# Layer 0's opening: key and rotary columns as one run of 288, in three chunks by contraction blocks

## The chip, the cores and the metric

The kernel runs on one core of a Trainium2 chip. The metric is the device time of one execution in microseconds (us); lower is better. Engines: PE multiplies matrices, DVE, ACT and POOL work on vectors, and SP issues most of the transfers from HBM, the chip's large memory. PEld is PE's loading of weights, which goes beside its matmuls.

## The reference

Two layers of a block with three parallel branches, over 256 latent tokens (x) and 256 context tokens (ctx), width 1024. Each layer scales and shifts its normalised input by vectors computed from a conditioning vector, then multiplies by one combined matrix `w_in` (1024 x 5024). The opening of layer 0 is this much of it:

```python
c_act = jax.nn.silu(c); cc_act = jax.nn.silu(c_ctx)
sh1, sc1, g1, sh2, sc2, g2 = jnp.split((c_act @ w_mod[l] + b_mod[l])[:, None, :], N_MOD, axis=-1)
mod_c = jnp.split(cc_act @ w_mod[l] + b_mod[l], N_MOD, axis=-1)
hc = modulate(rms_norm(xc, ln1_g[l]), mod_c[0], mod_c[1])
projc = hc @ w_in[l]
h = modulate(rms_norm(x, ln1_g[l]), sh1, sc1)
proj = h @ w_in[l]
# columns of proj: 0:384 queries, 384:640 keys and values (latent), 640:672 rotary key,
# 672:1184 the convolution's a and g, then the short convolution, then the gates
```

After it come attention with a rotary key, two convolution branches, a gated merge with an output projection, and a SwiGLU layer of width 2816, twice, and a last RMSNorm. Everything is float32.

## The kernel before

All activations are kept transposed, channels on the 128 partitions, the 2 x 256 tokens of both streams side by side (512 columns), in eight blocks of channels (`DT` = 8). To keep float32's accuracy a product is made of three: weights and activations are each split into a high part and a remainder, `Whi`, `Wlo`, `Hhi`, `Hlo`, and a tile gets `Whi`x`Hhi`, `Wlo`x`Hhi` and `Whi`x`Hlo` for each block.

Weights come in chunks. SP loads a chunk into one of four slots of `Wraw` (`load`, L450), ACT writes `Whi` (`split_hi`, L401), DVE writes `Wlo` (`split_lo`, L412), and PE takes it with `chunk()`. The kind of a chunk tells the two splits its shape: "plain" is 8 blocks x 128 columns, "rope" is 8 blocks x the 32 rotary columns; its high part and remainder lie side by side in `Whi`, 64 columns a block, so that one matmul makes both products (`rotation`, L2219 to L2222). A tile is one bank of PSUM, PE's output memory, 128 x 512; `tile_done` tells that it is complete.

The order of work is written out by hand, engine by engine; each engine runs its list in order, and semaphores tie the lists together. No planner is in it.

The opening computes the first vectors of the conditioning and the first tiles of the projection together. Shift and scale of the first norm are 2048 columns of `w_mod[0]`. They are taken in four parts; part p gives the vectors of the channel blocks 2p and 2p+1. A part is eight transfers of 256 KB, one for each block of the contraction, and PE multiplies them in four pairs (`first_pair`, L2379, 16 matmuls of 128 columns into `scores`). Then a serial chain: ACT copies the result as a row (`mod_row`, L824), PE turns it (`mod_turn`, L2422), DVE adds the bias (L1333), makes the gain (L1417) and the scaled input Z (L1431), ACT adds the shift and writes `Hhi` (L840), DVE writes `Hlo` (L1405). Only then can PE multiply by these two blocks.

In the time between, `opening` (from L2226) lets PE work on blocks that it has, for three tiles (two of the keys, the first of the convolution's g) and a fourth, rotary one. `high(j)` (L2235, L2236) multiplies block j's `Hhi` by `Whi` and `Wlo` of the tiles named, `low(j)` (L2242) its `Hlo` by `Whi`, `rotation` the rotary columns. `first_steps(p)` is the four pairs of part p one behind the other. After the opening come the other tiles of the projection, one by one (L2075 to L2077).

SP issues in this order: x, ctx, the two conditioning vectors, key tile 0, part 0, key tile 1, tile g, rotary columns, parts 1, 2 and 3, a table, and then the chunks of the other tiles, each as its slot comes free.

Of the kernel before, what the change touches and what calls it, by code (L numbers as in the profile page):

```python
# [17 lines left out]
P = 128  # L18
# [8 lines left out]
CW = P  # L27
# [36 lines left out]

HEAD_KINDS = ["keys", "fours", "values"]
# [98 lines left out]
def build(nc, x, c, ctx_in, c_ctx, w_mod, b_mod, ln1_g, w_in, q_a_norm_g, w_q_b, kv_a_norm_g,  # L166
# [6 lines left out]
    with stack:  # L173
# [165 lines left out]
        cond_tanh = sem("cond_tanh")  # L339
        cond_done = sem("cond_done")  # L340
        conv_a = sem("conv_a")
        conv_summed = sem("conv_summed")
# [14 lines left out]
        def parts(kind, slot):  # L357
# [81 lines left out]
        def _(sp):  # L439
# [335 lines left out]
        def _(act):  # L775
# [98 lines left out]
            act.activation(RSTD[:, :], PV[:, :], ACT.Copy).then_inc(x_norm, 1)  # L874
            look()
            mod_row(0)
            for l in range(DEPTH):
                TQ = NS[l] * SEQ
                nxt = ahead(projection_kinds(l), HEAD_KINDS)
                if l == 0:  # L880
                    next(nxt)
                    for part in range(PARTS):
                        normed_h(0, 0, 2, range(part * PART, (part + 1) * PART))
                        if part == 0:
                            look()
                            look()
# [14 lines left out]
                copy_out(TG[:, 0, 0:TQ], TQ, ACT.Tanh, 0.5)  # L901
                step_in()
                at.tile()
# [390 lines left out]
        def _(dve):  # L1294
# [230 lines left out]
            at.mod.n = TURN  # L1525
            look()
            dve.wait_ge(x_norm, 1)
            for l in range(DEPTH):
                TQ = NS[l] * SEQ
                nxt = ahead(projection_kinds(l), HEAD_KINDS)  # L1530
                if l == 0:
                    next(nxt)
                    for part in range(PARTS):
                        a, b = part * PART, (part + 1) * PART
                        mod_add_part(part)
                        gains(0, 0, LN1, 2, a, b)
                        normed_h(0, 0, 2, a, b)
                        if part == 0:
                            look()
                            look()  # L1540
                            look("rope")

# [3 lines left out]
                for j in range(2):  # L1546
                    if l or j:
                        step_in()
# [499 lines left out]
        def _(pe):  # L2048
# [163 lines left out]

            def rotation(slot, t, j, ready):

                both = Whi[:, slot, 0:DT * 2 * ROPE].rearrange("p (g n) -> p g n", g=DT)
                dst = banks[t.bank]
                pe.wait_ge(op_lo, ready + j + 1)
                if j == 0:
                    pe.matmul(dst[0:2 * ROPE, :], both[:, j, :], Hhi[:, j, :], start=True, stop=False)  # L2219
                last = pe.matmul(dst[0:ROPE, :], both[:, j, 0:ROPE], Hlo[:, j, :], start=False, stop=False)  # L2220
                if j:
                    last = pe.matmul(dst[0:2 * ROPE, :], both[:, j, :], Hhi[:, j, :], start=False, stop=j == DT - 1)  # L2222
                return last

            def opening(ready):

                slots = [chunk()]
                tiles = [new_tile() for _ in range(AHEAD)]

                def high(j, some=range(AHEAD)):  # L2230

                    pe.wait_ge(op_hi, ready + j + 1)
                    for q in some:
                        w, dst = slice(j * P, (j + 1) * P), banks[tiles[q].bank][:, :]
                        pe.matmul(dst, Whi[:, slots[q], w], Hhi[:, j, :], start=j == 0, stop=False)  # L2235
                        pe.matmul(dst, Wlo[:, slots[q], w], Hhi[:, j, :], start=False, stop=False)  # L2236

                def low(j, some=range(AHEAD)):

                    pe.wait_ge(op_lo, ready + j + 1)  # L2240
                    for q in some:
                        last = pe.matmul(banks[tiles[q].bank][:, :], Whi[:, slots[q], j * P:(j + 1) * P], Hlo[:, j, :],  # L2242
                                         start=False, stop=j == DT - 1)
                    return last

                high(0, [0])
                high(1, [0])
                low(0, [0])
                low(1, [0])
                first_pair(1, 0)  # L2250
                slots.append(chunk())
                high(0, [1])
                first_pair(1, 1)
                high(1, [1])
                first_pair(1, 2)
                slots.append(chunk())
                high(0, [2])
                first_pair(1, 3)
                low(0, [1, 2])
                mod_turn(1)  # L2260
                high(1, [2])
                low(1, [1, 2])
                slot, t = chunk(), new_tile()
                rotation(slot, t, 0, ready)
                rotation(slot, t, 1, ready)
                high(2)
# [12 lines left out]
                mod_turn(1)  # L2279
                high(5)  # L2280
                low(5)
                high(6)
                for q in range(AHEAD):
                    high(7, [q])
                    low(6, [q])
                    low(7, [q]).then_inc(tile_done, 1)
                rotation(slot, t, 6, ready)
                rotation(slot, t, 7, ready).then_inc(tile_done, 1)

# [172 lines left out]
            for l in range(DEPTH):  # L2462
# [23 lines left out]
                if l:  # L2486
                    slot, t = chunk(), new_tile()
                    for j in range(DT):
                        last = rotation(slot, t, j, o)
                    last.then_inc(tile_done, 1)  # L2490
# [330 lines left out]
```

## Time and profile before

| | us |
|---|---|
| median of 3 runs | 1224.73 (1224.48 to 1225.72) |
| profiled execution, its own time | 1224.44 |
| its span | 1222.7 |
| PE busy in the span | 1202.3 |
| DVE, ACT, POOL busy | 864.9, 530.0, 190.4 |

The span runs from the first instruction to the last; the execution's own time has a little around it. Every start below is in us from the span's start. PE is busy in nearly all of the span; the first of 40 slices of the page has seven tenths and the others nine or more. The page's chain that ended last is PE for 87% of the span.

### The profile page before, as it was taken

To read this page: it belongs to the slowest core of one execution; us is meant where nothing else is said; L and a number is where in the kernel's file an instruction comes from. 1 tells how busy PE (TensorE), PEld (TensorE's weight loads), DVE (VectorE), ACT (ScalarE), POOL (GpSimd) and SP (SyncE) were. 2 spreads that over 40 slices of the span, in tenths; PEclk is the share of its full clock that TensorE was granted. 3 is DMA by queue.
4 is the path that set the end of the run, shared out by engine and by line. 5 is a ranking of instruction groups with operands and counts; after the bars stand their busy time and mean duration, and the time that the engine had idled before them with its cause. 6 is when DMAs were issued, how large, how long until landed. Compare 5 with 4: busy or idle time off the path is not lost.

```text
span 1222.7 us, 17823 instructions
## 1 busy us (share of the span) xinstructions
PE 1202.3 (98%) x6842; PEld 1000.4 (82%) x6842; DVE 864.9 (71%) x1286; ACT 530.0 (43%) x891; POOL 190.4 (16%) x158
## 2 busy tenths in 40 slices
PE   7999999999999999999999999999999999999997
PEld 5677777788888898888888888889879998888886
DVE  4665866586877487678755665789887877766666
ACT  4342555522433352312232222465664555655554
POOL 0005994000001200000000000302980002000000
PEclk9999999999999999999999999999999999999999
DMA  9947322134464536557664665335434674676662
GB/s 297 314 142 216 84 54 69 35 87 121 120 172 124 169 92 198 159 156 215 185 201 144 211 195 161 93 98 147 124 111 115 168 209 141 195 200 189 181 198 88
DMA packets 265252, 188.88 MB, mean 154 GB/s; under 512 B 16035, under 2 KB 250833, under 8 KB 265169
## 3 DMA queue, kind: packets, MB, share of 16 engines
q1 hardware_dynamic: 264832, 187.60, 52.6%
q8 instruction: 55, 0.90, 0.3%
q14 instruction: 28, 0.23, 0.1%
q10 hardware_dynamic: 337, 0.15, 0.0%
HBM read 186.67 MB, written 1.05 MB: 154 GB/s over the span
## 4 chain that ended last, share of the span: by engine, by line
PE 87%; DVE 4%; ACT 3%; DMA 2%; issue 1%; DVEq 0%; ACTq 0%; SPq 0%
PE bank L2075 17%; PE bank L2077 17%; PE bank L2076 17%; PE bank L2116 5%; PE bank L2114 3%; PE scores L2563 3%; PE bank L2543 2%; PE bank L2545 2%; PE bank L2544 2%; PE probsT L2572 2%; PE attended L2586 1%; ACT Whi L401 1%; DMA Wraw<-in_w_in 1%; DVE Wlo L412 1%; PE bank L2642 1%
## 5 line engine op out<-in xcount | busy, mean ns | idle before, releaser
L412 DVE TENSOR_TENSOR Wlo<-Wraw,Whi 128x1024 fp32r<-128x1024 f32 (+3 forms) x294 | 321.7, 1103 | 105.4 <-ACT Whi L401 104.3
L401 ACT ACTIVATE Whi<-Wraw 128x1024 fp32r<-128x1024 f32 (+1 forms) x296 | 270.3, 928 | 127.0 <-PE bank L2077 71.6
L2075 PE MATMUL bank<-Hhi,Whi 128*128 128x512 f32 (+1 forms) x786 | 285.9, 364 | 0.4
L2076 PE MATMUL bank<-Hlo,Whi 128*128 128x512 f32 (+1 forms) x786 | 282.1, 359 | 0.0
L2077 PE MATMUL bank<-Hhi,Wlo 128*128 128x512 f32 (+1 forms) x786 | 282.0, 359 | 0.0
L2075 PEld LDWEIGHTS bank<-Hhi,Whi 128*128 128x128 f32 x786 | 148.6, 189 | 29.1 <-issue 6.4
L2076 PEld LDWEIGHTS bank<-Hlo,Whi 128*128 128x128 f32 x786 | 148.6, 189 | 22.3 <-issue 1.0
L2077 PEld LDWEIGHTS bank<-Hhi,Wlo 128*128 128x128 f32 x786 | 148.6, 189 | 21.9
L2075 PE MATMUL bank<-Uhi,Whi 128*128 128x512 f32 (+1 forms) x350 | 128.5, 367 | 0.2 <-issue 0.2
L2077 PE MATMUL bank<-Uhi,Wlo 128*128 128x512 f32 (+1 forms) x350 | 126.8, 362 | 0.0
L2076 PE MATMUL bank<-Ulo,Whi 128*128 128x512 f32 (+1 forms) x350 | 126.7, 362 | 0.0
L669 POOL TENSOR_TENSOR SUM<-SUM,V 128x512 f32<-128x512 f32 (+1 forms) x23 | 32.4, 1408 | 533.8 <-ACT V L795 533.6
L2116 PE MATMUL bank<-Hhi,Whi 128*128 128x512 f32 x287 | 102.4, 397 | 0.0
L718 POOL TENSOR_SCALAR SUM<-U,PAR 128x512 f32<-128x512 f32 (+1 forms) x56 | 81.1, 1448 | 62.1 <-DVE ACC L1597 56.8
L2114 PE MATMUL bank<-Hhi,Wlo 128*128 128x256 f32 x328 | 84.8, 279 | 0.0
L2075 PEld LDWEIGHTS bank<-Uhi,Whi 128*128 128x128 f32 x350 | 66.1, 189 | 11.6 <-issue 2.0
L2077 PEld LDWEIGHTS bank<-Uhi,Wlo 128*128 128x128 f32 x350 | 66.1, 189 | 10.2
L2076 PEld LDWEIGHTS bank<-Ulo,Whi 128*128 128x128 f32 x350 | 66.2, 189 | 10.0 <-issue 0.2
L1844 DVE SCALAR_TENSOR_TENSOR X<-bank,MOD,X 128x256 f32<-128x256 f32 x64 | 28.2, 479 | 55.3 <-PE bank L2077 52.9
L721 POOL TENSOR_TENSOR ACC<-ACC,SUM 128x512 f32<-128x512 f32 (+1 forms) x56 | 64.6, 1154 | 4.7
L785 ACT ACTIVATE V<-bank 128x512 f32<-128x512 f32 (+1 forms) x48 | 24.3, 507 | 93.9 <-PE bank L2077 92.4
L1346 DVE SCALAR_TENSOR_TENSOR G<-ATT,CV,G 128x1024 f32<-128x1024 f32 x50 | 64.8, 1320 | 0.0
(305 smaller groups left out, 1979.4 us busy)
## 6 DMA issues: line engine op xcount, KB each, us to landing
Wraw<-in_w_ff SPq DMA_DIRECT2D x126, 512.0 KB, 3.9
Wraw<-in_w_in SPq DMA_DIRECT2D x78, 512.0 KB, 4.0
ATT<-in_w_mod SPq DMA_DIRECT2D x58, 512.0 KB, 4.5
Wraw<-in_w_o SPq DMA_DIRECT2D x16, 512.0 KB, 4.0
ACC<-in_w_mod SPq DMA_DIRECT2D x14, 512.0 KB, 4.6
Wraw<-in_w_mla_o SPq DMA_DIRECT2D x8, 512.0 KB, 4.1
ATT<-in_w_mod SPq DMA_DIRECT2D x12, 256.0 KB, 7.6
Wraw<-in_w_kv_b SPq DMA_DIRECT2D x12, 256.0 KB, 3.7
```

Source lines behind the costliest of these rows:

```text
L401: last = act.activation(hi, raw, ACT.Copy)
L412: last = eng.tensor_tensor(lo, raw, hi.bitcast(F32), ALU.subtract)
L669: pool.tensor_tensor(SUM[:, 0:n], SUM[:, 0:n], SQ[:, slot, 0:n], ALU.add).then_inc(sq_summed, 1)
L718: v = mark(pool.tensor_scalar(by_stream(SUM[:, :], l), U[:, 1, 0:NS[l], w:w + SEQ], PAR[:, l, CDW + 2 * w + 1:CDW + 2 * w + 2], None, ALU. ...
L721: ins = pool.tensor_tensor(by_stream(ACC[:, 1, :], l), by_stream(ACC[:, 1, :], l), by_stream(SUM[:, :], l), ALU.add)
L1346: last = dve.scalar_tensor_tensor(acc(s), raw, c, acc(s), mult, add)
L2075: pe.matmul(dst, sh, mh, start=j == 0, stop=False)
L2076: pe.matmul(dst, sh, ml, start=False, stop=False)
L2077: last = pe.matmul(dst, sl, mh, start=False, stop=j == k - 1)
L2114: last = pe.matmul(banks[t.bank][:, half[0]], Wlo[:, slot, w], Hhi[:, j, half[0]], start=False, stop=False)
L2116: last = pe.matmul(banks[t.bank][:, :], Whi[:, slot, w], Hhi[:, j, :], start=False, stop=j == DT - 1)
L2563: pe.matmul(S[h][:, 0:kt * P], Qb[0:NOPE + ROPE, h, col:col + P], Kb[0:NOPE + ROPE, h, k0 * P:(k0 + kt) * P], start=True, stop=True).then_ ...
```

## The change

The two key tiles and the rotary columns lie side by side in `w_in`: 128 + 128 + 32 = 288 columns. Before, they were three chunks, each with all eight blocks of the contraction. Now they are loaded as one run of 288 columns, in three chunks by blocks: 0 to 2, 3 to 5 (kind "wide") and 6 and 7 ("rest"). Tile g stays a chunk of its own. SP issues the three between the parts of the conditioning. ACT and DVE split each in its turn, each in two instructions, since key and rotary columns are laid out differently. In `opening` PE takes both key tiles together from the start, and the pairs of parts 2 and 3 stand between the matmuls instead of one behind the other. `rotation` gets its weights from the caller. As the first chunk's last use comes early (rotation of block 2, which now counts up `first_rows`), ACT splits the chunk of the tile after the opening before the first tile is complete; the splits of the next ones wait for the third and fourth tile.

```diff
+RUN = 3
+WIDE = 2 * CW + ROPE
...
+            if kind in ("wide", "rest"):
+                n, full = RUN if kind == "wide" else DT - 2 * RUN, WIDE + ROPE
+                raw = Wraw[:, slot, 0:n * WIDE].rearrange("p (k n) -> p k n", k=n)
+                hi, lo = (w[:, slot, 0:n * full].rearrange("p (k n) -> p k n", k=n) for w in (Whi, Wlo))
+                return [(raw[:, :, 0:2 * CW], hi[:, :, 0:2 * CW], lo[:, :, 0:2 * CW]),
+                        (raw[:, :, 2 * CW:WIDE], hi[:, :, 2 * CW:WIDE], hi[:, :, WIDE:full])]
...
-            project(0, 0)
+            def rows_of_keys(k0, n):
+                load(w_in[0], k0 * P, n, KV0, WIDE)
+
+            rows_of_keys(0, RUN)
...
                 if part == 0:
-                    for n in range(1, AHEAD + 1):
-                        project(0, n)
+                    project(0, 2)
+                if part == 1:
+                    rows_of_keys(RUN, RUN)
+                if part == 2:
+                    rows_of_keys(2 * RUN, DT - 2 * RUN)
...
                         normed_h(0, 0, 2, range(part * PART, (part + 1) * PART))
-                        if part == 0:
-                            look()
-                            look()
-                            look("rope")
+                        if part == PARTS - 1:
+                            act.wait_ge(first_rows, 1)
+                            look(next(nxt))
+                        else:
+                            look(("plain", "wide", "rest")[part])
...
                 for j in range(2):
-                    if l or j:
+                    if l:
                         step_in()
                     t = at.tile()
                     act.wait_ge(tile_done, t.done)
                     square(banks[t.bank][:, :], T, j, 2)
+                if l == 0:
+                    act.wait_ge(tile_done, at.tiles.now() + 1)
                 step_in()
...
-                low(2)
-                first_steps(2)
-                rotation(slot, t, 2, ready)
+                rotated(1)
+                high(2, both)
+                first_pair(2, 0)
+                high(2, [2])
+                first_pair(2, 1)
+                low(2)
+                first_pair(2, 2)
+                rotated(2).then_inc(first_rows, 1)
+                first_pair(2, 3)
+                rows.append(chunk())
+                high(3, both)
                 mod_turn(1)
-                high(3)
+                high(3, [2])
                 low(3)
-                rotation(slot, t, 3, ready)
+                rotated(3)
                 high(4)
+                first_pair(3, 0)
+                first_pair(3, 1)
                 low(4)
-                rotation(slot, t, 4, ready)
-                first_steps(3)
-                rotation(slot, t, 5, ready)
+                first_pair(3, 2)
+                high(5, both)
+                first_pair(3, 3)
+                high(5, [2])
                 mod_turn(1)
-                high(5)
                 low(5)
+                rotated(4)
+                rotated(5)
+                rows.append(chunk())
                 high(6)
```

How SP's list of transfers moves. Before, from the first chunk to part 2 (ATT and PR hold part 0, ACC, BG, U and C part 1, G part 2):

```order
L450 DMA Wraw<-in_w_in 128x8x128
L493 DMA ATT<-in_w_mod 128x2x256 x6
L493 DMA PR<-in_w_mod 128x2x256 x2
L450 DMA Wraw<-in_w_in 128x8x128 x2
L450 DMA Wraw<-in_w_in 128x8x32
L493 DMA ACC<-in_w_mod 128x2x256 x2
L493 DMA BG<-in_w_mod 128x2x256 x2
L493 DMA U<-in_w_mod 128x2x256 x2
L493 DMA C<-in_w_mod 128x2x256 x2
L493 DMA G<-in_w_mod 128x2x256 x8
```

And now:

```order
L460 DMA Wraw<-in_w_in 128x3x288
L506 DMA ATT<-in_w_mod 128x2x256 x6
L506 DMA PR<-in_w_mod 128x2x256 x2
L460 DMA Wraw<-in_w_in 128x8x128
L506 DMA ACC<-in_w_mod 128x2x256 x2
L506 DMA BG<-in_w_mod 128x2x256 x2
L506 DMA U<-in_w_mod 128x2x256 x2
L506 DMA C<-in_w_mod 128x2x256 x2
L460 DMA Wraw<-in_w_in 128x3x288
L506 DMA G<-in_w_mod 128x2x256 x8
L460 DMA Wraw<-in_w_in 128x2x288
```

Between part 0 and part 1 stands one transfer instead of three; the others went behind parts 1 and 2.

How PE's list moves in the second round, from the last tile's `low(2)` on. Before, with part 2's pairs (`scores<-G`) and the transpose that ends them (`probsT`); 4 wide matmuls of `high(2)` stand ahead of the first row shown:

```order
L2235 MATMUL bank<-Hhi,Whi 128x512
L2236 MATMUL bank<-Hhi,Wlo 128x512
L2242 MATMUL bank<-Hlo,Whi 128x512 x3
L2379 MATMUL scores<-G,CV 32x128 x32
L2220 MATMUL bank<-Hlo,Whi 32x512
L2222 MATMUL bank<-Hhi,Whi 64x512
L2422 MATMUL probsT<-IDN,ATT 128x128
```

And now, from behind the 4 wide matmuls of `high(2, both)`:

```order
L2423 MATMUL scores<-G,CV 32x128 x8
L2263 MATMUL bank<-Hhi,Whi 128x512
L2264 MATMUL bank<-Hhi,Wlo 128x512
L2423 MATMUL scores<-G,CV 32x128 x8
L2271 MATMUL bank<-Hlo,Whi 128x512 x3
L2423 MATMUL scores<-G,CV 32x128 x8
L2240 MATMUL bank<-Hlo,Whi 32x512
L2242 MATMUL bank<-Hhi,Whi 64x512
L2423 MATMUL scores<-G,CV 32x128 x8
```

Behind this follow four wide matmuls of `high(3, both)`, and only then the transpose. The pairs, which stood together, stand apart, and 15 wide matmuls stand ahead of the transpose instead of 11. A row of 8 in these lists is a pair; the trace shows each of its matmuls as two.

## Rows read from the trace of the kernel before

**Rows 1.** The page: busy us (share of the span), instructions of each engine.
```profile
PE 1202.3 (98%) x6842; PEld 1000.4 (82%) x6842; DVE 864.9 (71%) x1286; ACT 530.0 (43%) x891; POOL 190.4 (16%) x158
```
**Rows 2.** Busy time by stretch (columns in the first row), the opening's four rounds.
```profile
core 0: us, PE busy (x) PEld busy (x) DVE busy (x) ACT busy (x) POOL busy (x), PEclk, DMA share, GB/s
22.60:33.23 10.63, 9.30 (x87) 4.87 (x87) 6.27 (x16) 4.09 (x9) 2.42 (x3) 1.00 1.02 333
33.23:40.62 7.39, 7.39 (x88) 5.54 (x89) 3.88 (x14) 2.14 (x6) 0.00 (x0) 1.00 1.10 353
40.62:48.19 7.57, 7.43 (x88) 5.28 (x88) 3.57 (x13) 1.84 (x6) 0.00 (x0) 1.00 1.13 301
48.19:53.67 5.48, 5.34 (x22) 3.79 (x22) 3.74 (x8) 3.61 (x6) 0.00 (x0) 1.00 0.99 357
```
**Rows 3.** Timeline, PE, round 2 (start, us, engine, line, instruction, count).
```profile
33.23 0.50 PE L2235 MATMUL bank<-Hhi,Whi 128*128 128x512 f32 x1 [0.37 <-ACT Hhi L840]
...
33.57 0.40 PE L2236 MATMUL bank<-Hhi,Wlo 128*128 128x512 f32 x1
...
34.73 0.84 PE L2242 MATMUL bank<-Hlo,Whi 128*128 128x512 f32 x3
35.50 1.96 PE L2379 MATMUL scores<-G,CV 128*32 128x128 f32 x64
37.38 0.42 PE L2220 MATMUL bank<-Hlo,Whi 128*32 128x512 f32 x1
37.64 0.39 PE L2222 MATMUL bank<-Hhi,Whi 128*64 128x512 f32 x1
```
**Rows 4.** Timeline, all engines: the chain between rounds 2 and 3.
```profile
37.94 0.30 PE L2422 MATMUL probsT<-IDN,ATT 128*128 128x128 f32 x1
...
38.28 0.23 DVE L1333 TENSOR_TENSOR MOD<-probsT,PAR 128x4 f32<-128x4 f32 x2 [3.26 <-PE probsT L2422]
...
39.51 1.71 ACT L840 ACTIVATE Hhi<-Z,MOD 128x256 fp32r<-128x256 f32 x4 [1.71 <-DVE Z L1431]
...
40.47 0.19 PEld L2235 LDWEIGHTS bank<-Hhi,Whi 128*128 128x128 f32 x1 [0.18 <-ACT Hhi L840]
```
**Rows 5.** Timeline, PE and ACT, part 1's pairs in round 1.
```profile
24.77 0.38 PEld L2379 LDWEIGHTS scores<-ACC,CV 128*32 128x32 f32 x16 [0.24 <-issue]
...
25.85 0.40 PE L2236 MATMUL bank<-Hhi,Wlo 128*128 128x512 f32 x1
26.18 0.64 PE L2379 MATMUL scores<-BG,CV 128*32 128x128 f32 x16
26.75 0.50 PE L2235 MATMUL bank<-Hhi,Whi 128*128 128x512 f32 x1
27.09 0.40 PE L2236 MATMUL bank<-Hhi,Wlo 128*128 128x512 f32 x1
...
28.07 0.64 PE L2379 MATMUL scores<-U,CV 128*32 128x128 f32 x16 [0.58 <-DMA U<-in_w_mod]
...
29.58 0.65 PE L2379 MATMUL scores<-C,CV 128*32 128x128 f32 x16 [0.21 <-DMA C<-in_w_mod]
...
30.29 0.28 ACT L824 ACTIVATE ATT<-scores 128x128 f32<-128x128 f32 x1 [4.84 <-PE scores L2379]
...
30.73 0.29 PE L2422 MATMUL probsT<-IDN,ATT 128*128 128x128 f32 x1
```
**Rows 6.** Busy time by stretch: 512-byte rows flow, w_mod's 1 KB rows, 128-byte rows.
```profile
7.80:9.90 2.10, 1.75 (x14) 1.29 (x14) 2.10 (x7) 1.29 (x5) 0.00 (x0) 1.00 1.14 303
10.00:15.50 5.50, 3.39 (x25) 2.58 (x24) 4.38 (x19) 4.13 (x7) 0.00 (x0) 1.00 1.11 341
...
19.00:21.00 2.00, 1.60 (x26) 1.33 (x23) 0.46 (x4) 0.28 (x1) 0.00 (x0) 1.00 0.72 143
```
**Rows 7.** Timeline, PE: part 0's last pair and the opening's first matmul.
```profile
18.87 0.65 PE L2379 MATMUL scores<-PR,CV 128*32 128x128 f32 x16 [0.88 <-DMA PR<-in_w_mod]
...
22.60 0.47 PE L2235 MATMUL bank<-Hhi,Whi 128*128 128x512 f32 x1
```
**Rows 8.** Timeline, the opening's end and the next tile.
```profile
50.81 0.60 ACT L795 ACTIVATE V<-bank 128x512 f32<-128x512 f32 x1 [1.87 <-PE bank L2242]
...
51.30 1.05 ACT L401 ACTIVATE Whi<-Wraw 128x1024 fp32r<-128x1024 f32 x1
...
52.39 1.23 DVE L412 TENSOR_TENSOR Wlo<-Wraw,Whi 128x1024 fp32r<-128x1024 f32 x1 [0.19 <-ACT Whi L401]
...
53.67 0.19 PEld L2075 LDWEIGHTS bank<-Hhi,Whi 128*128 128x128 f32 x1 [0.64 <-DVE Wlo L412]
```

More of the change, by code:

```diff
@@ L874, in _ @@
             act.activation(RSTD[:, :], PV[:, :], ACT.Copy).then_inc(x_norm, 1)
-            look()
+            look("wide")
             mod_row(0)
@@ L1525, in _ @@
             at.mod.n = TURN
-            look()
+            look("wide")
             dve.wait_ge(x_norm, 1)
@@ L1537, in _ @@
                         normed_h(0, 0, 2, a, b)
[L1538 to L1541, printed above, removed]
+                        if part == PARTS - 1:
+                            look(next(nxt))
+                        else:
+                            look(("plain", "wide", "rest")[part])
                 def step_in():
@@ L2211, in staggered_tiles, with rotation @@
                     half_product(tiles[2], slots[2], DT, H, 0, DT - 1, DT, ready).then_inc(tile_done, 1)
[L2213 to L2215 removed]
+            def rotation(both, t, j, ready):
                 dst = banks[t.bank]
@@ L2218, in rotation, with columns, weights @@
                 if j == 0:
-                    pe.matmul(dst[0:2 * ROPE, :], both[:, j, :], Hhi[:, j, :], start=True, stop=False)
-                last = pe.matmul(dst[0:ROPE, :], both[:, j, 0:ROPE], Hlo[:, j, :], start=False, stop=False)
+                    pe.matmul(dst[0:2 * ROPE, :], both, Hhi[:, j, :], start=True, stop=False)
+                last = pe.matmul(dst[0:ROPE, :], both[:, 0:ROPE], Hlo[:, j, :], start=False, stop=False)
                 if j:
-                    last = pe.matmul(dst[0:2 * ROPE, :], both[:, j, :], Hhi[:, j, :], start=False, stop=j == DT - 1)
+                    last = pe.matmul(dst[0:2 * ROPE, :], both, Hhi[:, j, :], start=False, stop=j == DT - 1)
                 return last
             def opening(ready):
-                slots = [chunk()]
-                tiles = [new_tile() for _ in range(AHEAD)]
+                rows, tiles = [chunk()], [new_tile() for _ in range(AHEAD + 1)]
+                def columns(j, a, n):
+                    a += j % RUN * (WIDE + ROPE)
+                    return rows[j // RUN], slice(a, a + n)
+                def weights(q, j):
+                    return columns(j, q * CW, CW) if q < 2 else (single, slice(j * P, (j + 1) * P))
                 def high(j, some=range(AHEAD)):
@@ L2233, in high @@
                     for q in some:
-                        w, dst = slice(j * P, (j + 1) * P), banks[tiles[q].bank][:, :]
-                        pe.matmul(dst, Whi[:, slots[q], w], Hhi[:, j, :], start=j == 0, stop=False)
-                        pe.matmul(dst, Wlo[:, slots[q], w], Hhi[:, j, :], start=False, stop=False)
+                        (slot, w), dst = weights(q, j), banks[tiles[q].bank][:, :]
+                        pe.matmul(dst, Whi[:, slot, w], Hhi[:, j, :], start=j == 0, stop=False)
+                        pe.matmul(dst, Wlo[:, slot, w], Hhi[:, j, :], start=False, stop=False)
                 def low(j, some=range(AHEAD)):
@@ L2241, in low @@
                     for q in some:
-                        last = pe.matmul(banks[tiles[q].bank][:, :], Whi[:, slots[q], j * P:(j + 1) * P], Hlo[:, j, :],
+                        slot, w = weights(q, j)
+                        last = pe.matmul(banks[tiles[q].bank][:, :], Whi[:, slot, w], Hlo[:, j, :],
                                          start=False, stop=j == DT - 1)
                     return last
-                high(0, [0])
-                high(1, [0])
-                low(0, [0])
@@ L2249, in opening, with rotated @@
-                low(1, [0])
+                def rotated(j):
+                    slot, w = columns(j, 2 * CW, 2 * ROPE)
+                    return rotation(Whi[:, slot, w], tiles[AHEAD], j, ready)
+                both = [0, 1]
+                high(0, both)
+                high(1, both)
                 first_pair(1, 0)
-                slots.append(chunk())
-                high(0, [1])
+                low(0, both)
+                low(1, both)
                 first_pair(1, 1)
-                high(1, [1])
+                rotated(0)
@@ L2255, in opening @@
                 first_pair(1, 2)
-                slots.append(chunk())
+                single = chunk()
                 high(0, [2])
                 first_pair(1, 3)
-                low(0, [1, 2])
+                high(1, [2])
                 mod_turn(1)
[L2261 to L2266, printed above, removed]
-                low(2)
@@ L2279, in opening @@
+                high(5, [2])
                 mod_turn(1)
-                high(5)
                 low(5)
+                rotated(4)
+                rotated(5)
+                rows.append(chunk())
                 high(6)
-                for q in range(AHEAD):
-                    high(7, [q])
-                    low(6, [q])
+                high(7)
+                low(6, both)
+                for q in both:
                     low(7, [q]).then_inc(tile_done, 1)
-                rotation(slot, t, 6, ready)
@@ L2288, in opening @@
-                rotation(slot, t, 7, ready).then_inc(tile_done, 1)
+                low(6, [2])
+                low(7, [2]).then_inc(tile_done, 1)
+                rotated(6)
+                rotated(7).then_inc(tile_done, 1)
             def first_tiles(ns, ready, before={}, inside={}, ops=normed):
@@ L2487, in _ @@
                     slot, t = chunk(), new_tile()
+                    both = Whi[:, slot, 0:DT * 2 * ROPE].rearrange("p (g n) -> p g n", g=DT)
                     for j in range(DT):
-                        last = rotation(slot, t, j, o)
+                        last = rotation(both[:, j, :], t, j, o)
                     last.then_inc(tile_done, 1)
```

8 lines of the change are left out of this document (6 added, 2 removed).

## The prediction

> **What bounds the kernel now.** I read the page's busy shares first: PE is busy 98% of the span [rows 1], in the opening at full granted clock [rows 2], so only time in which PE stands, or is made to do more, can move the end. Next, the chain of waits. From 53.67 us, where the first tile after the opening starts, it runs through matmul after matmul of layer 0's projection; what the opening gains or loses before 53.67 is carried to the end nearly whole, since the weight loads that come later (slots free, then a transfer) are themselves tied to PE's progress. So the question is when the first matmul of that tile starts.
>
> The opening falls into four rounds, each set by one piece of conditioning (a quarter of w_mod's first 2048 columns): part 1, 2, 3 and the last, at 22.60, 33.23, 40.62 and 48.19 us; they take 10.63, 7.39, 7.57 and 5.48 us [rows 2]. A round has 22 wide matmuls (512 columns) and, in the first three, a part's eight w_mod blocks, which the kernel takes in four pairs of 16 small matmuls. Wide matmuls start every 0.232 us: five steps from 33.57 to 34.73 [rows 3]. Each round ends in one serial chain, PE transpose, DVE MOD, AV and Z, ACT Hhi, next wide matmul: 37.94 to 40.47, 2.53 us [rows 4] (30.73 to 33.23 is 2.50). While it runs PE needs other work.
>
> Where does PE stand now? In round 1 it waits for w_mod's data ahead of the pairs from U and C, which start at 28.07 and 29.58 [rows 5]. 22 x 0.232 = 5.1, four pairs 3.1 and the transpose 0.1 leave 2.3 us of the 10.63 idle. Rounds 2 and 3 have next to none: 22 x 0.232 = 5.10, four pairs together 1.98, transpose and restarts some 0.3, in all 7.4 of 7.39 and 7.57. Before the projection PE waits a little for Wlo [rows 8].
>
> **Part by part: the transfers.** The bytes are the same (1.18 MB in rows of 1152 bytes in place of 1.05 MB in rows of 512 bytes and 0.13 MB in rows of 128 bytes; the single block of 0.52 MB stays), but fewer stand ahead of part 1, and none of 128 bytes. The trace has 303 GB/s while 512-byte rows flow, 341 GB/s for w_mod's 1 KB rows, and 143 GB/s about the 128-byte rows [rows 6]. The first chunk falls from 0.524 MB at 303 (1.73 us) to 0.442 MB at 341, the nearest row (1.30): part 0 lands 0.43 us sooner. The last pair of part 0 is what the start waits for (PE idle until PR's data, 18.87 [rows 7]), so the opening starts 0.45 us sooner, at 22.15. Bounds: 0 (landing is set by something else) and 0.6 (1152-byte rows as much faster again as 1 KB rows are than 512-byte ones).
>
> The Trainium skill ("DMA: Bandwidth & Descriptors", section "Measured (HBM→SBUF, 128 partitions, SWDGE, issued from GpSimd)") speaks against smaller chunks: it wants 1 MiB per transfer and has 138 GB/s at 64 KB against 341 GB/s at 1 MB. By its lower figure the first chunk would take 3.2 us, and the sum would be 1.9 us higher. The trace does not bear it out here: w_mod's pieces are 256 KB each and flow at 341 GB/s back to back.
>
> After part 0 (data at 18.3) the single block takes 1.7 us and each pair 0.524 MB at 341, 1.54 us: part 1's pairs are there at 21.6, 23.1, 24.7 and 26.2. PE reaches them at 24.2, 25.9, 27.1 and 28.4 (below), so no wait for data is left in round 1. Part 2 follows one chunk of 1.3 us later (29.0 to 33.7, wanted from 33.2 to 37.2), part 3 after 0.295 MB more (36.1 to 40.7, wanted from 42.8). SP issues in the new order without a new wait; only its transfer for slot 3 waits for a split made later (about 44 us), for a tile wanted after 70.
>
> **Round 1.** What is late next is PE itself. Before the transpose the new order has 18 wide matmuls and four pairs standing alone. What a pair alone costs: 25.85 to 26.18 to it instead of 0.232, 0.57 for itself (26.18 to 26.75), 0.34 for the next step (26.75 to 27.09) instead of 0.232: 0.10 + 0.57 + 0.10 = 0.77 us [rows 5]. Sum 18 x 0.232 + 0.08 (first step) + 4 x 0.77 + 0.07 = 7.41 us. The other bound, the last pair's start + 0.71 for ACT's copy + 0.44 for the transpose as in 29.58, 30.29, 30.73, comes to 7.35. Before it was 30.73 - 22.60 = 8.13. Gain 0.72; round 2 starts at 22.15 + 7.41 + 2.50 = 32.06.
>
> **Round 2, the main term.** Four pairs together cost 35.50 to 37.38, with 0.07 before and 0.03 after: 1.98 [rows 3]. Spread one by one they cost 4 x 0.77 = 3.08, so 1.10 more. And the transpose moves back: ahead of it stood 9 wide matmuls, the pairs and 2 of rotation; now 15 wide ones. New: 15 x 0.232 + 0.11 + 3.08 + 0.07 = 6.74 to the transpose, + 2.53 of chain = 9.27. The work behind the transpose (2 + 3 + 2 matmuls, 1.7 us) doesn't fill the chain, so PE stands 0.7 us. Before, 7.39: loss 1.88. Nothing pays for it, since there was no wait for data in this round. Bounds: 0 (the pairs' edges hide behind weight loads and the chain is covered) and 2.7 (a pair alone costs 0.24 more, the idle of a weight load beside the first pair [rows 5]).
>
> **Round 3.** Two pairs together, then two alone: 0.77 + 0.47 + 1.54 = 2.78 against 1.98. 15 x 0.232 + 0.10 + 2.78 + 0.07 = 6.43, + 2.53 = 8.96, against 7.57: loss 1.39, bounds 0 and 2.1.
>
> **Round 4 and what follows.** 22 wide matmuls, 5.10 + 0.10 = 5.20. The 0.3 us for tile 4's Wlo goes, because ACT now splits that chunk as soon as the rotation of block 2 is done, not after the first tile and a square [rows 8]. Against 5.48 a gain of 0.28. The next conversions come after the third and fourth tile, with 5.5 us of matmuls and a total over them, so I cost them at nothing; without that cover each is 2.3 us (ACT 1.05, DVE 1.24).
> Edits on ACT and DVE (two instructions instead of one for a chunk of three blocks, 288 x 3 elements instead of 1024) stand behind Hhi and Hlo of their round with over 3 us to spare: nothing, either way 0.1.
>
> **Sum.** -0.45 - 0.72 + 1.88 + 1.39 - 0.28 = +1.82 us: the projection starts at 55.49 instead of 53.67. On the profiled span of 1222.7 that is 1224.5; this execution's own time is 1224.44, so 1226.3; the median of the runs shown stands 0.3 above it, so 1226.5 us. A change of 0.2%, 2.45 us, is about what a measurement of this kernel can tell from none: the forecast is "no change that can be told", on the slow side.
>
> **Rivals.**
> A, the pairs' edges hide: PE's queue gets through a pair alone as cheaply as four together, and the transpose's place is covered. Then rounds 2 and 3 cost nothing: -0.45 - 0.72 - 0.28 = -1.45, 1223.3 us. For it: weight loads overlap matmuls in the trace (PEld 1000.4 of PE's 1202.3 us [rows 1]). Against: the steps of 0.33 and 0.57 us are measured beside such a pair. 0.16.
> B, the transfers were the bound in all rounds: all of the 2.3 idle goes, the start and round 4 give 0.7, and rounds 2 and 3 no loss: 1221.7 us. For it: the DMA share is full in every round [rows 2]. Against: PE starts part 2's pairs at 35.50 with no wait for data. 0.06.
> C, the edges cost more than a rested PE showed and the head start fails: in rounds 2 and 3 the pairs never follow a rest, each alone adds a weight load's exposed 0.24 (6 of them, 1.4), and landing is not sooner (+0.45): +3.7, 1228.4 us. It decides once the spread pairs in round 2 cost over 0.95 us each with the start at 22.6. For it: "issue" idle ahead of weight loads beside pairs. Against: the pair from BG had waited only 0.1 us. 0.20.
> D, the smaller chunk flows slowly, at the 143 GB/s that the trace has about the 128 KB transfer [rows 6]: 0.442 MB take 3.1 us, the opening starts 1.4 later instead of 0.45 sooner, +3.6, 1228.3 us. Against: w_mod's still smaller pieces at 341 GB/s. 0.03. (It is the way in which the rule of the Trainium skill, "DMA: Bandwidth & Descriptors", told above, would work here.)
>
> **How the numbers follow.** Forecast 0.55 (1225.6 to 1227.6; of this 0.05 lies above 0.2%), A 0.16, B 0.06, C 0.20, D 0.03. Faster by over 0.2%: B and an edge of A, 0.08. Slower: C, D and 0.05 of the forecast, 0.28. Within: 0.64. The range leaves out B and the tails of C and D: 1222.9 to 1228.7.
>
> **What would show it.** Right: first wide matmul near 22.2; no PE wait for a DMA in round 1; transposes near 29.6, 38.8 and 47.8; round 2 lasting 9.3 and round 3 9.0 us; 0.6 us of PE waiting for Hhi at the start of rounds 3 and 4; no wait for Wlo near 55.5. Wrong: a DMA named as releaser of PE from round 1 on; rounds 2 and 3 of 7.4 us (A); a start at or after 22.6 (C, D); a wait on ACT or DVE splits of the new chunks, which I cost at nothing.

## The result and the profile after

The changed kernel takes 1228.98 us (median of 7, 1228.80 to 1229.87), the kernel before 1225.60 in the same runs: ratio 1.0035 (95% interval 1.0025 to 1.0044). It is slower by 4.3 us by the ratio, by 3.4 between these two medians, where the forecast was 1226.5 and "no change that can be told". The seven executions fall into two groups: four take 1228.8 to 1229.0 at a mean granted clock of 0.997 or 0.998, three take 1229.7 to 1229.9 at 0.995. The profiled one, 1229.86, is of the second; its span is 1227.9 against 1222.7.

The rounds first. Busy time by stretch of the changed kernel, columns as in [rows 2], whose four rows these answer:

```profile
25.20:34.99 9.79, 8.50 (x87) 4.93 (x87) 4.81 (x14) 2.85 (x7) 2.42 (x3) 1.00 1.10 352
34.99:44.08 9.09, 8.48 (x87) 5.04 (x87) 4.75 (x15) 2.89 (x8) 0.00 (x0) 1.00 1.07 311
44.08:53.03 8.95, 8.25 (x88) 5.14 (x88) 4.55 (x15) 2.75 (x8) 0.00 (x0) 1.00 0.49 133
53.03:58.24 5.21, 5.21 (x22) 3.78 (x23) 3.65 (x8) 3.09 (x6) 0.00 (x0) 1.00 0.96 335
```

They last 9.79, 9.09, 8.95 and 5.21 us; the prediction had 9.91, 9.27, 8.96 and 5.20. The first column's start is what went wrong: 25.20, not 22.15. From there on the projection is 4.57 us later than before (58.24 against 53.67).

Timeline of the changed kernel, PE, up to the opening; it answers to [rows 7]:

```profile
12.36 1.16 PE L2493 MATMUL attended<-ROOT,ONES 128*128 128x128 f32 x8 [0.80 <-DVE ROOT L1530]
14.38 0.47 PE L2498 MATMUL bank<-IDN,V 95*128 95x95 f32 x3 [0.86 <-DMA V<-in_sc_dw]
15.95 2.93 PE L2475 MATMUL scores<-ONES 128*128 128x128 f32 x12 [1.10 <-DVE CV L1544]
18.81 2.79 PE L2423 MATMUL scores<-ATT,CV 128*32 128x128 f32 x48
21.37 0.73 PE L2423 MATMUL scores<-PR,CV 128*32 128x128 f32 x16
...
25.20 0.47 PE L2263 MATMUL bank<-Hhi,Whi 128*128 128x512 f32 x1
```

And of the kernel before, the same place:

```profile
13.37 0.44 PE L2454 MATMUL bank<-IDN,V 95*128 95x95 f32 x3
14.91 1.61 PE L2431 MATMUL scores<-ONES 128*128 128x128 f32 x12 [1.10 <-DVE CV L1523]
16.45 1.54 PE L2379 MATMUL scores<-ATT,CV 128*32 128x128 f32 x48
```

Read them side by side. The transposes of the parameter vectors (L2498, L2454 before) wait for V<-in_sc_dw, the last of ten small transfers that ACT issues, and start 1.0 us later; so does all behind them, CV included. Then the same 12 small matmuls take 2.93 us instead of 1.61, and the 48 of part 0 2.79 instead of 1.54. That is the clock. Busy time by stretch, the changed kernel (the clock is the third number from the end):

```profile
13.00:14.00 1.00, 0.51 (x5) 0.32 (x3) 0.37 (x2) 0.59 (x2) 0.00 (x0) 1.00 1.11 344
14.00:15.00 1.00, 0.47 (x3) 0.28 (x3) 0.12 (x1) 0.20 (x2) 0.00 (x0) 0.89 1.11 348
15.00:16.00 1.00, 0.05 (x1) 0.05 (x1) 0.82 (x5) 0.96 (x2) 0.00 (x0) 0.50 1.15 322
20.00:21.00 1.00, 1.00 (x28) 0.92 (x24) 0.00 (x0) 0.00 (x0) 0.00 (x0) 0.50 1.14 352
22.00:23.00 1.00, 0.59 (x8) 0.50 (x5) 0.06 (x1) 0.28 (x1) 0.00 (x0) 1.00 1.10 352
```

0.50 is 1.2 GHz, 1.00 is 2.4 GHz. The fall comes late in the stretch 14 to 15 (0.89), about when the transposes end. Before it PE had stood for 0.80 us ahead of L2493 and 0.86 us ahead of the transposes; the 1.1 us for CV follow. In the kernel before the clock is 1.00 in all these stretches. Part 0's data, for which PE stood until 18.87 in [rows 7], is no longer waited for: the pair from PR starts at 21.37 without a wait for a DMA. It did land sooner: PR's second transfer landed at 18.8 in the kernel before (issued at 11.0, 7.8 us to land) and at 18.1 in the changed one (9.0 and 9.0, both rounded).

Why do the vectors land late? The transfer views of both kernels, one stretch of 1 us each. Columns: queue, packets, MB, share; q1 is SP's queue, q10 the one of ACT. The kernel before, 8 to 9 us, then 12 to 13:

```profile
q1 hardware_dynamic: 600, 0.30, 107.7%
q10 hardware_dynamic: 47, 0.02, 6.8%
...
q1 hardware_dynamic: 346, 0.33, 108.4%
q10 hardware_dynamic: 18, 0.01, 3.2%
```

The changed kernel, 8 to 9, 12 to 13, and 13 to 14:

```profile
q1 hardware_dynamic: 343, 0.37, 103.2%
q10 hardware_dynamic: 35, 0.01, 4.8%
...
q1 hardware_dynamic: 335, 0.32, 104.7%
q10 hardware_dynamic: 28, 0.01, 5.6%
...
q1 hardware_dynamic: 350, 0.34, 108.2%
q10 hardware_dynamic: 19, 0.01, 3.2%
```

Both have 337 packets of vectors to move. While the first chunk's 512-byte packets flow, SP's queue moves 600 packets in a microsecond and the other 47; with 1152-byte packets 343 and 35. Before, the vectors' queue runs empty within the stretch 12 to 13; now it still moves 19 packets in the next.

### The profile page after: what moved, and what is told of

Read it like the earlier page. It is cut to its first block and busy times, and to the rows that moved or that the text cites. A ratio compares the mean times of both kernels' runs of the same rounds, so it can differ in the third digit from the quotient of the medians.

```text
span 1227.9 us, 17830 instructions
## 1 busy us (share of the span) xinstructions
PE 1206.4 (98%) x6842; PEld 1002.1 (82%) x6842; DVE 865.9 (71%) x1289; ACT 530.6 (43%) x894; POOL 189.0 (15%) x158
## 5 line engine op out<-in xcount | busy, mean ns | idle before, releaser
L411 ACT ACTIVATE Whi<-Wraw 128x1024 fp32r<-128x1024 f32 (+5 forms) x299 | 270.9, 921 | 127.3 <-PE bank L2098 71.9
```

Of the source, the lines that this page charges most:

```text
L411: last = act.activation(hi, raw, ACT.Copy)
```

## The experiments

Each time stands beside its ratio to the kernel before, run on the same chip; e1 to e4 share a chip, e5 to e8 another, e9 to e12 a third. P, S and the like name theories in the expectations. The round starts are read from each timeline as above.

**e1**: the changed kernel once more, no edit.

> The changed kernel unchanged, for a second profile. Its first one has the opening's first wide matmul at 25.20 us instead of 22.60, after the vectors' last transfer (V<-in_sc_dw) landed at 14.4, 1.0 later than it was wanted, and PE ran at half clock from 14.8 to 21.7. Theory S (the late start belongs to the change: SP's first chunk has 384 rows instead of 1024, so SP runs ahead and the vectors queue behind more of w_mod): the transfer is again the releaser of the transposes near 14.4, the start again at 24 to 25.5, rounds 1 to 3 again 9.8, 9.1, 9.0 us, time 1228.8 to 1229.9. Rival J (chance of one execution): the start falls back to 22.2 to 22.7 at full clock in this profile and the time to about 1226.5.

1228.55 us, ratio 1.0032 (1.0020 to 1.0045). Not chance: the start is at 23.91, rounds of 9.8, 9.1, 8.9 and 5.2, and again

```profile
14.16 0.47 PE L2498 MATMUL bank<-IDN,V 95*128 95x95 f32 x3 [0.56 <-DMA V<-in_sc_dw]
15.73 2.26 PE L2475 MATMUL scores<-ONES 128*128 128x128 f32 x12 [1.10 <-DVE CV L1544]
```

The clock fell later than in the first profile, past 16 us, and for half as long; in 15 to 20 us it was 0.66. So the start is 1.3 to 2.6 us late. Rival J falls in its form: the start does not fall back to 22.7 in a second profile.

**e2**: rounds 2 and 3 back in the old order.

```diff
-                high(2, both)
-                first_pair(2, 0)
...
-                high(5, [2])
-                mod_turn(1)
-                low(5)
-                rotated(4)
-                rotated(5)
-                rows.append(chunk())
+                high(2)
+                low(2)
+                first_steps(2)
+                rotated(2).then_inc(first_rows, 1)
+                rows.append(chunk())
+                mod_turn(1)
+                high(3)
+                low(3)
+                rotated(3)
+                high(4)
+                low(4)
+                rotated(4)
+                first_steps(3)
+                rotated(5)
+                mod_turn(1)
+                high(5)
+                low(5)
+                rows.append(chunk())
```

> Only PE's list in rounds 2 and 3 is put back: parts 2 and 3 in four pairs one behind the other, the transposes where they stood before. Transfers, splits and round 1 as in the changed kernel. Theory P (spread pairs and the later transpose cost what the rounds' sum says): rounds 2 and 3 fall from 9.1 and 9.0 to 7.4 and 7.6 us, 3.1 in all, time 1225.8 for 1228.9. Rival Q (the pairs were spread because data or splits of the new chunks come late): the time falls by less than 1 us, and PE waits for a DMA or for Wlo in rounds 2 and 3.

1225.59 us, ratio 1.0011 (1.0002 to 1.0020), 3.0 below e1. Rounds 9.80, 7.39, 7.66, 5.19. P holds: the new data was there for the old order, and the order alone cost 3.0 us. The profiled execution, 1226.81, is one of the five longer of eleven; in it the clock fell a second time, at 1033 us (below, behind e12).

**e3**: the first chunk in short rows.

```diff
-            rows_of_keys(0, RUN)
+            at.chunk.next()
+            for i, (a, n) in enumerate(((0, CW), (CW, CW), (2 * CW, ROPE))):
+                sp.dma_start(Wraw[:, 0, 0:RUN * WIDE].rearrange("p (k n) -> p k n", k=RUN)[:, :, a:a + n],
+                             w_in[0][0:RUN * P, KV0 + a:KV0 + a + n].rearrange("(k p) n -> p k n", p=P)).then_inc(
+                                 more_rows if i else raw_in[0], 16)
```

> The first chunk of key and rotary columns comes in three transfers of 512-, 512- and 128-byte rows (1152 rows in all) instead of one with 384 rows of 1152 bytes; same bytes, same place, all else as in the changed kernel. Theory S (many rows hold SP back, so that the vectors, issued by ACT, queue behind less): the vectors land about 13.3, PE stays at full clock, the start goes back to 22.5 to 23 us and the time falls by 2 to 3 us to about 1226.5. Rival R (the late vectors have nothing to do with the first chunk's rows): vectors again at 14.4, start at 25, and the time the same or 0.5 higher.

1227.81 us, ratio 1.0025 (1.0014 to 1.0036), 0.7 below e1. Half of theory S: the vectors are back in time (the 12 matmuls behind CV start at 14.98), start 23.14. But the clock still fell:

```profile
14.98 2.93 PE L2481 MATMUL scores<-ONES 128*128 128x128 f32 x12 [1.10 <-DVE CV L1550]
17.84 1.77 PE L2429 MATMUL scores<-ATT,CV 128*32 128x128 f32 x48
```

ACT's queue is empty in the whole stretch 12 to 13. So the first chunk's form moves the vectors' landing, and R falls; it is not the whole of the clock. The run changes two things at once, the length of the rows and the number of transfers (three for one).

**e4**: ACT issues the vectors before anything else.

```diff
-            act.wait_ge(consts, 2)
-            load_sqrt()
             act.dma_start(PST[0:2 * NMOD * DT, 0, 2 * P:3 * P],
...
+            act.wait_ge(consts, 2)
+            load_sqrt()
             for _ in range(2 * DT):
```

> ACT issues its ten small transfers of vectors ahead of its wait for the constants and its table load; all else as in the changed kernel. Theory S: the last is issued 0.6 us sooner and has less of w_mod ahead, lands at 12.9 to 13.8 instead of 14.4, and if PE's pause stays short enough for the full clock the start falls to 22.5 to 23.3, the time by 1.5 to 3 us. Rival K (the pause of PE between the transposes and the first matmul by CV, not the landing, brings the clock down): the start falls by no more than the landing, 0.5 to 1 us, at half clock from about 14 to 21.

1227.78 us, ratio 1.0021 (1.0011 to 1.0032). The transposes start at 14.15, as in e1, and the start is 23.89: K is nearer. ACT's queue still moves 11 packets in the stretch 13 to 14. The profile shows no gain at the start. The median is 0.8 below e1's: three of the eight executions take 1226.8 to 1227.0 at a mean granted clock of 0.999, the other five 1227.6 to 1229.1 at 0.996 to 0.998. No profile in which the clock fell here has a mean above 0.998, so those three may have kept it; none of them was profiled.

**e5**: the kernel before once more, no edit.

> The kernel before, unchanged, for a second profile. Question: does the clock of PE between 15 and 20 us belong to the kernel or to the execution? Theory C (the change brings it: all five profiles of kernels with the new transfers granted 0.66 or less in 15 to 20 us): the clock is 1.00 there again, the first wide matmul at 22.6, the 3.2 us later part between 804 and 1208 the same. Rival J (chance of an execution): 0.66 or less here too, and the first wide matmul at 23 to 24.

1224.81 us, ratio 0.9996. Clock 1.00 in 15 to 20 us, start 22.75, a wait until 19.01 for PR's data. Theory C, as far as two profiles go (0.998 and 0.999 on average over the span). But the executions without a profile leave J open: of 92 of the kernel before in the runs of e1 to e12, 17 have a mean granted clock of 0.995 or 0.996 and take 1225.5 to 1226.6, about 1 us above the median of the others. Where their clock fell no trace shows. This profile has 0.36 us more than the first profile between 833 and 866 us; so such steps of about 0.36, which the changed kernel's profile also has (at 764 to 818 and at 833 to 866), belong in part to the execution.

**e6**: the two pauses filled in the changed kernel.

```diff
+            keep_busy(3)
             pe.wait_ge(vec_in, 16 * N_VEC)
...
+            keep_busy(4)
             pe.wait_ge(cond_done, 1)
             keep_busy(BEFORE_STEPS)
```

> The changed kernel with 3 more warming matmuls of PE ahead of its wait for the vectors and 4 more ahead of its wait for CV, which fill the two pauses (about 0.8 and 1.1 us) before part 0's pairs. Theory C (the pauses cost the clock, and the half clock the late start): clock 1.00 in 15 to 20 us, first wide matmul at 22.2 to 22.8 instead of 23.9, rounds 9.8, 9.1, 9.0, 5.2 as before, time about 1.2 lower, 1227.3. Rival L (the vectors' late landing costs the start by itself): start at 23.5 or later at full clock, and the time falls by under 0.5.

1227.26 us, ratio 1.0020 (1.0011 to 1.0029). C holds:

```profile
13.43 0.83 PE L2475 MATMUL scores<-ONES 128*128 128x128 f32 x6
...
14.66 1.08 PE L2475 MATMUL scores<-ONES 128*128 128x128 f32 x8
15.93 1.60 PE L2475 MATMUL scores<-ONES 128*128 128x128 f32 x12 [0.19 <-DVE CV L1544]
17.47 1.52 PE L2423 MATMUL scores<-ATT,CV 128*32 128x128 f32 x48
18.80 0.62 PE L2423 MATMUL scores<-PR,CV 128*32 128x128 f32 x16
...
22.51 0.47 PE L2263 MATMUL bank<-Hhi,Whi 128*128 128x512 f32 x1
...
55.51 0.47 PE L2096 MATMUL bank<-Hhi,Whi 128*128 128x512 f32 x1
```

CV is as late as in the first profile, yet the same 12 and 48 matmuls take 1.60 and 1.52 us, and the start is at 22.51. The clock was what made the start late, 1.4 us against e1 with vectors as late, and rival L falls. The projection starts at 55.51, 1.41 before e1 and 1.84 after the kernel before. In time the ratios of e1 and e6 lie 1.5 us apart, on two chips and with intervals that overlap, so the 1.4 us rest on the profiles.

**e7**: the same two edits in the kernel before.

> The kernel before with the same 3 and 4 warming matmuls. Theory C: where the clock is 1.00 anyway they change nothing, 1224.7 within 0.5, start 22.6. Rival J: they mend a half clock that the kernel before has in some executions, and the median falls by 0.5 to 1.

1224.76 us, ratio 1.0000 (0.9991 to 1.0009): nothing at the median. Start 22.50. Rival J is not settled by it: of the 66 executions of e6 to e11, all with the idle matmuls, none has a mean granted clock below 0.997 (17 of 92 of the kernel before have). So the kernel before may lose its clock at this place in some executions too.

**e8**: e2 and e6 together, and round 1 in a new order.

```diff
                 high(0, both)
-                high(1, both)
                 first_pair(1, 0)
-                low(0, both)
-                low(1, both)
+                high(1, both)
                 first_pair(1, 1)
-                rotated(0)
                 first_pair(1, 2)
+                low(0, both)
+                first_pair(1, 3)
                 single = chunk()
                 high(0, [2])
-                first_pair(1, 3)
-                high(1, [2])
                 mod_turn(1)
+                high(1, [2])
+                low(1, both)
                 low(0, [2])
                 low(1, [2])
+                rotated(0)
                 rotated(1)
```

> New transfers and splits; rounds 2 and 3 in the old order (pairs together, transposes early); the warming matmuls of e6; and round 1 anew: the pairs of part 1 as early as their data should allow, the transpose behind 12 wide matmuls instead of 18, so that 10 fill the chain behind it. By the sums: start 22.4, round 1 12 x 0.232 + 3 x 0.77 + 0.47 + 0.15 + 2.5 = 8.2 us (9.8 in the changed kernel), rounds 2 to 4 7.4, 7.6 and 5.2, projection at 50.8 instead of 53.67, time 1221.8, a gain of 2.9 on the kernel before. Rival D (the data of part 1 comes at PE's old pace, the last pair at 29.5 as in the kernel before): PE waits for U or C, round 1 takes 9.8 or more, time 1223.5 or above.

1222.56 us, ratio 0.9978 (0.9969 to 0.9987): faster than both kernels, 2.7 us below the kernel before by the ratio. Start 22.56, rounds 8.14, 7.38, 7.67, 5.19, projection at 50.94. D falls: the last pair of part 1 starts at 27.03 with no wait for a DMA, where [rows 5] had a wait until 29.58:

```profile
25.36 0.65 PE L2414 MATMUL scores<-BG,CV 128*32 128x128 f32 x16
25.82 0.62 PE L2414 MATMUL scores<-U,CV 128*32 128x128 f32 x16
...
27.03 0.64 PE L2414 MATMUL scores<-C,CV 128*32 128x128 f32 x16
...
28.18 0.29 PE L2457 MATMUL probsT<-IDN,ATT 128*128 128x128 f32 x1
```

**e9**: in e8, SP holds w_mod back until x has landed.

```diff
             rows_of_keys(0, RUN)
+            sp.wait_ge(x_in[0], 16)
             for part in range(PARTS):
```

> e8 with one wait more on SP: it issues part 0 of w_mod only once x has landed (about 5.6 us), so that the vectors, issued by ACT until 5.9, queue behind less. Theory S: the vectors land before 13.3 without a wait of PE for V<-in_sc_dw, CV comes at 14.9 to 15.2 instead of 16.0, part 0's data sets the start as the prediction had it: first wide matmul at 22.0 to 22.3 instead of 22.56, time 0.3 to 0.5 lower, 1222.1. Rival R (the vectors' landing has nothing to do with how far SP ran ahead): a wait for V<-in_sc_dw near 14.4 again, the start at 22.5 or later, since the held transfers come later too.

1222.43 us, ratio 0.9977 (0.9968 to 0.9986), no difference from e8. SP issued w_mod from 5.80 instead of 3.10, and CV still came at 16.0, the start at 22.58. The idle matmuls would have held the transposes until about 14.2 in any case (e7), but the queue tells the same: ACT's still moves 21 packets in the stretch 13 to 14, in e8 20. So it is not how much of w_mod stands ahead of the vectors; the theory S falls in this form, and only e3's finding stays, that the form of the first chunk counts. That the two queues take turns by packets fits the counts of 600 beside 47 and 343 beside 35, but no run isolates it. The Trainium skill ("DMA: Bandwidth & Descriptors", "Rules for kernel authors") says that rings of two issuing engines are packet-interleaved on the 16 DMA engines.

**e10**: in e6, the transposes of rounds 2 and 3 moved ahead, the pairs left spread.

```diff
                 first_pair(2, 1)
-                low(2)
+                low(2, [0])
                 first_pair(2, 2)
-                rotated(2).then_inc(first_rows, 1)
+                low(2, both[1:] + [2])
                 first_pair(2, 3)
-                rows.append(chunk())
-                high(3, both)
+                rotated(2).then_inc(first_rows, 1)
                 mod_turn(1)
-                high(3, [2])
+                rows.append(chunk())
+                high(3)
...
                 first_pair(3, 2)
-                high(5, both)
+                rotated(4)
                 first_pair(3, 3)
-                high(5, [2])
+                rotated(5)
                 mod_turn(1)
+                high(5)
                 low(5)
-                rotated(4)
-                rotated(5)
```

> e6 (the changed kernel with the warming matmuls) with the pairs of rounds 2 and 3 still spread, but the two transposes moved ahead of high(3, both) and high(5), behind 11 and 13 wide matmuls. Theory P (a lone pair costs 0.77 us, and the transposes' place the rest): round 2 takes 11 x 0.232 + 0.11 + 3.08 + 0.07 and then 11 wide matmuls, 8.5 us (9.09 in e6), round 3 8.5 (8.95), time 1.05 lower than e6, 1226.2; what is left to e2's rounds, 2.0 us, is the spreading. Rival Q (only the place of the transposes cost time): rounds of 7.5 to 7.8, time 1224.7.

1225.74 us, ratio 1.0005 (0.9996 to 1.0014). Rounds 2 and 3 take 8.48 and 8.26 us; in e6 they take 9.09 and 8.94, in e11 7.39 and 7.66. So of the 2.98 us the transposes' place cost 1.29 and the spreading 1.69: 1.09 in round 2, where the prediction had 1.10, and 0.60 in round 3, where it had 0.80.

**e11**: e2 and e6 together, round 1 as in the changed kernel.

> e2 (rounds 2 and 3 in the old order) with the warming matmuls of e6; round 1 as in the changed kernel. Theory P + C: start 22.5, rounds 9.8, 7.4, 7.6, 5.2, projection at 52.5 instead of 53.67, time 3.0 lower than e6, 1224.2, between the kernel before and e8; e8's round 1 is then worth 1.6 us. Rival: under 0.5 apart from e8, that is, round 1's order is worth nothing.

1224.27 us, ratio 0.9992 (0.9983 to 1.0001). Start 22.57, projection at 52.61, 1.06 before the kernel before and 1.67 after e8: that is round 1's new order.

**e12**: e3 once more, in one execution.

> e3 once more, for the clock alone. In e3 PE's pauses ahead of part 0's pairs were as long as in the kernel before, and the clock still fell. Theory C1 (the pauses alone decide, near their limit, so that it is chance): the clock is 1.00 in 15 to 20 us this time in one case of two, and the first wide matmul at 22.3 to 22.6. Theory C2 (something of the new transfers decides): 0.66 and 23.1 again.

1229.19 us in its one execution. The vectors are in time again, and the clock falls again:

```profile
13.58 0.41 PE L2504 MATMUL bank<-IDN,V 95*128 95x95 f32 x3
15.09 2.93 PE L2481 MATMUL scores<-ONES 128*128 128x128 f32 x12 [1.10 <-DVE CV L1550]
```

The start is at 23.10 and the projection at 56.12, as in e3; the rest of the time came later in the span. The pause ahead of CV ends at 15.09 here, at 15.07 in e5, and is as long; e5 kept the clock. By C1, chance, two falls out of two come in one case of four, so it is less likely but not excluded; what it would be in the new transfers that counts is open as well.

A second fall speaks for chance. In e12 (at 1035 us) and in e2 (at 1033) the clock also fell in the second layer, in code that the change does not touch; PE's matmuls behind it are some 1.1 us later against the kernel before than those ahead of it. e2, the pause ahead of it and a stretch in it:

```profile
1031.71 0.36 PE L2150 MATMUL bank<-Hhi,Whi 128*128 128x256 f32 x1 [1.83 <-ACT Hhi L856]
1034.00:1035.00 1.00, 1.00 (x6) 1.00 (x6) 0.90 (x3) 0.52 (x2) 0.00 (x0) 0.50 0.00 0
```

And the kernel before, with the same pause and the full clock:

```profile
1030.63 0.36 PE L2129 MATMUL bank<-Hhi,Whi 128*128 128x256 f32 x1 [1.82 <-ACT Hhi L840]
1033.00:1034.00 1.00, 1.00 (x11) 1.00 (x10) 0.88 (x2) 0.53 (x2) 0.00 (x0) 1.00 0.00 0
```

The other profiles with the same code have the full clock there. So the same work can keep the clock in one execution and lose it in another.

## Why the prediction was wrong

**The step that failed is the start**: "so the opening starts 0.45 us sooner, at 22.15". It was 1.31 us later in e1 and 2.60 in the first profile. The working took the last pair of part 0 for what the start waits for, since that was so in [rows 7], and asked only when its data would come. It left out the other arm of the same join, the chain from the vectors to CV, and that this chain hangs on a queue of small transfers beside the chunk that it was resizing. Its bounds, 0 and 0.6 us sooner, had no end on the late side. This term alone, 1.76 us off in e1 and 3.05 in the profile, carries the time out of the range. The chain from the vectors is the small part of it: with the clock held (e6) the start is at 22.51, 0.36 late. The rest, 1.40 us in e1 and 2.69 in the profile, is PE's granted clock ahead of the opening, 1.2 instead of 2.4 GHz for 3.4 and 6.8 us. The prediction had read the clock of the kernel before, 1.00 in [rows 2] and [rows 6], and took it over for the changed kernel without a reason. The pauses take part in the fall, since filling them held the clock in five profiles of five; what decides whether a kernel with these pauses loses it, the new transfers or the execution, stays open. With the clock held the projection starts at 55.51, and the prediction said 55.49. That agreement has two small errors in it: the start 0.36 later, the rounds 0.34 shorter.

**Part 0 no longer sets the start.** Its data lands sooner, as predicted, and by 0.7 us (18.1 for 18.8) rather than 0.43, but PE no longer waits for it. In e6, e8 and e9 CV sets the start, at 15.9 to 16.0: PE reaches PR's pair at 18.8 to 18.9, some 0.8 us behind the data.

**Round 1** right: predicted 9.91, 9.8 in every run with this order. PE waits for no transfer in it.

**Rounds 2 and 3** right: losses of 1.88 and 1.39 predicted, 1.70 and 1.38 in the profile, 3.0 undone by e2. The two parts of that, spreading and place, are both real (e10). The idle of 0.6 us ahead of Hhi at the start of rounds 3 and 4 is there (0.61 and 0.70).

**Round 4** right: 5.21 for 5.20; there is no wait for Wlo, and PE waits for no split of the new chunks.

**The sum** of the rounds: +2.27 predicted, +1.97 in the profile (33.04 against 31.07). The shift of 4.5 us stays the same until 764 us, so what the opening loses is carried on whole, as assumed; 0.7 more comes later, in two steps of about 0.36, of which a second profile of the kernel before has one (e5).

**The rivals.** A and B fall with the rounds of 9.09 and 8.95 us, which e2 and e10 take apart. C came out nearest in time, 1228.4, for a wrong reason: the pairs cost no more than forecast, and what failed besides the head start was the clock. D's time, 1228.3, is as near and its sign, a start at or after 22.6, came true, yet it falls: SP's queue moves 0.37 MB in the stretch 8 to 9, where the new chunk flows.

## What to carry to other kernels

Where several arms meet in one start, work out each arm, not only the one that came last in the trace: a faster last arm hands the start to the next, and a change to transfers can move that one too. Small matmuls spread among wide ones cost their edges each time (1.09 us for four groups in round 2, about 0.27 each), and a transpose that starts a serial chain belongs ahead of the work that can cover the chain: pairs early and in blocks, ten wide matmuls behind the transpose and idle matmuls in the two pauses made the same new transfers 2.7 us faster than the old kernel instead of 4.3 slower. And where PE pauses twice shortly before serial work, a few idle matmuls in the pauses are a cheap insurance: in the kernel before they cost nothing at the median (e7).

## What the hardware showed that I had not expected

The granted clock fell, at pauses of PE of 0.6 to 1.1 us with little work between (behind 0.80 and 0.86 us in the profile after; behind 1.01 and 1.10 in e3), from 2.4 to 1.2 GHz for 3.4 to 7 us, and the same 48 small matmuls took up to 2.79 us instead of 1.54. Seven idle matmuls in the pauses kept the clock at 1.00 in all five kernels that had them beside the new transfers (e6, e8 to e11). All six profiles of the new transfers without them lost it; the two of the kernel before did not, though the pauses of e5 (1.01 and 1.10 us) are those of e3. Pauses alone do not tell the two apart, and the second fall in e2 and e12 shows that the same work can go either way.

The form of one big transfer on one queue (384 rows of 1152 bytes, or 1152 shorter rows in three transfers) moved the landing of small transfers on another by about 1 us (e3), while starting the big transfers behind it 2.7 us later did not (e9).
